# Where the down weights stand in the order of weight loads of a mixture-of-experts loop

## What is computed

```python
def expert_block(args):
    xb, e = args
    hid = jax.nn.silu(xb @ w_gate[e]) * (xb @ w_up[e])
    return hid @ w_down[e]
```

## Time and profile before

| | |
|---|---|
| median of 3 runs | 1393.48 us (1389.54 to 1395.79) |
| profiled execution | 1391.97 us |
| its span | 1389.9 us |
| TensorE matmuls busy | 1292.5 us (93%) |
| VectorE busy | 559.7 us (40%) |
| ScalarE busy | 351.2 us (25%) |
| GpSimd busy | 160.5 us (12%) |
| read from HBM | 299.49 MB |
| down weights, issue to landing, median | 30.5 us |
| gate/up weights, issue to landing, median | 26.8 us |

### The profile page before, as it was taken

The page is one execution under the profiler, slowest core; times in us unless marked ns, Lnnn a source line. Parts: engine busy times, 40 slices in busy tenths (PEclk is TensorE's granted clock), DMA queues, the critical chain, the costliest instruction groups (busy, mean ns, idle before and its releaser), DMA issues.

```text
span 1389.9 us, 21101 instructions
## 1 busy us (share of the span) xinstructions
PE 1292.5 (93%) x7560; PEld 640.0 (46%) x7561; DVE 559.7 (40%) x1034; ACT 351.2 (25%) x759; POOL 160.5 (12%) x278
## 2 busy tenths in 40 slices
PE   5999999999999998999999998999999987897777
PEld 1445656568954444554445545433333333332222
DVE  1366363655214333349786635312212212121115
ACT  1223231422135442221467510101111101110102
POOL 4011010101120000000000001411121111111110
PEclk9999999999999999999999999999999999999999
DMA  9250704323163110014112384789999999999995
GB/s 365 84 212 11 279 26 167 138 79 149 35 187 147 46 46 1 0 49 167 52 57 76 122 348 182 276 350 396 411 412 419 399 406 421 403 402 416 409 391 209
DMA packets 40420, 303.93 MB, mean 219 GB/s; under 512 B 7964, under 2 KB 8116, under 8 KB 22800
## 3 DMA queue, kind: packets, MB, share of 16 engines
q1 hardware_dynamic: 31808, 285.12, 52.3%
q0 software_dynamic: 8528, 17.67, 4.1%
HBM read 299.49 MB, written 13.75 MB: 225 GB/s over the span
## 4 chain that ended last, share of the span: by engine, by line
PE 74%; DMA 14%; DVE 6%; issue 2%; ACT 2%; POOL 1%; DVEq 0%; SPq 0%; ACTq 0%; POOLq 0%
PE bank L858 21%; PE bank L2874 12%; DMA arena<-in_w_down 11%; PE bank L790 8%; PE bank L2892 7%; PE bank L904 4%; PE bank L969 2%; PE bank L847 2%; PE bank L2862 2%; DMA arena<-in_ada_w 1%; PE bank L1186 1%; PE bank L1130 1%; PE bank L1107 1%; PE bank L893 1%; PE bank L2883 1%
## 5 line engine op out<-in xcount | busy, mean ns | idle before, releaser
L858 PE MATMUL bank<-hT,arena 128*128 128x512 f32 x720 | 320.0, 599 | 0.0
L2874 PE MATMUL bank<-arena,hT 128*64 128x512 f32 x1024 | 231.9, 603 | 18.0 <-DMA arena<-in_w_gu 17.6
L858 PEld LDWEIGHTS bank<-hT,arena 128*128 128x128 f32 x720 | 135.0, 191 | 162.6 <-issue 159.2
L2874 PEld LDWEIGHTS bank<-arena,hT 128*64 128x64 f32 x1024 | 72.9, 138 | 156.3 <-issue 138.1
L2892 PE MATMUL bank<-arena,yT 128*64 128x512 f32 x512 | 123.8, 628 | 15.7 <-DMA arena<-in_w_down 13.9
L790 PE MATMUL bank<-arena,yT 128*128 128x512 f32 x256 | 114.5, 601 | 2.4 <-DVE yT L1685 2.3
L3062 DVE TENSOR_SCALAR hT<-hT 128x256 f32<-128x256 f32 x32 | 9.4, 295 | 248.4 <-ACT hT L3000 248.4
L3000 ACT ACTIVATE hT<-bank 128x256 f32<-128x256 f32 x32 | 12.3, 384 | 264.0 <-PE bank L2874 264.0
L790 PEld LDWEIGHTS bank<-arena,yT 128*128 128x128 f32 x256 | 48.1, 192 | 60.0 <-issue 56.2
L2892 PEld LDWEIGHTS bank<-arena,yT 128*64 128x64 f32 x512 | 36.1, 143 | 78.7 <-issue 61.2
L904 PEld LDWEIGHTS bank<-arena 64*64 64x64 f32 x1856 | 59.3, 135 | 23.8 <-issue 14.4
(11 more groups left out here) (489 smaller groups left out, 1609.1 us busy)
## 6 DMA issues: line engine op xcount, KB each, us to landing
arena<-in_w_gu SPq DMA_DIRECT2D x63, 2048.0 KB, 26.8
arena<-in_w_down SPq DMA_DIRECT2D x32, 2048.0 KB, 30.5
arena<-in_w_in SPq DMA_DIRECT2D x53, 512.0 KB, 4.6
arena<-in_ada_w SPq DMA_DIRECT2D x24, 1024.0 KB, 5.1
arena<-in_w_ada SPq DMA_DIRECT2D x8, 1024.0 KB, 9.1
arena<-in_w_out SPq DMA_DIRECT2D x8, 1024.0 KB, 9.0
arena<-in_w_ada SPq DMA_DIRECT2D x8, 512.0 KB, 4.7
arena<-expert_rows SPq DMA_DIRECT2D x4, 1024.0 KB, 8.4
```

Source lines behind the costliest of these rows:

```text
L858: last = T.matmul(bank[0:rows, :], w[:, k, 0:rows], hT[:, k, :], start=k == 0, stop=k == KD - 1)
L2874: last = T.matmul(banks[1 + ub][MT * h:MT * h + MT, :], tile.xT[:, k, :], wgu[u][:, k // 4, k % 4, :, 256 * h:256 * h + 256], start=k == 0 ...
```

## The change

`next_gate_up` gets an argument `between`, which is called after half 0 has been asked for and ahead of the waits for half 1. `body` passes `next_down` there instead of calling it afterwards. Where down already went first (e = 4, 5, 30), nothing moves. For e = 31 there is no next gate/up, and `next_down` is called as before. So SyncE's order in a body is now: half 0 of gate/up of e+1, down of e, half 1 of gate/up of e+1.

```diff
@@ -2701,7 +2701,7 @@
-            def next_gate_up(u, e):
+            def next_gate_up(u, e, between=None):
 
                 p, n = slot_before(e)
                 eng.wait_ge(first.half_done, p + 1)
@@ -2709,6 +2709,8 @@
                 eng.wait_ge(more_.half_done, n + 1)
                 stand_alone(eng)
                 load_half(u, e, 0)
+                if between:
+                    between()
                 eng.wait_ge(first.gate_up, p + 2)
                 stand_alone(eng)
                 eng.wait_ge(more_.gate_up, n + 1)
@@ -2730,10 +2732,10 @@
                 down_first = isinstance(e, int) and (e == NE - 2 or e in (U + 1, U + 2))
                 if down_first:
                     next_down()
-                if not (isinstance(e, int) and e == NE - 1):
-                    next_gate_up(after(it, u)[1], e + 1)
-                if not down_first:
+                if isinstance(e, int) and e == NE - 1:
                     next_down()
+                else:
+                    next_gate_up(after(it, u)[1], e + 1, None if down_first else next_down)
```

## The result

The changed kernel takes 1399.11 us (median of 20 runs, 1393.16 to 1402.87), the kernel before 1393.76 us (20 runs, 1389.54 to 1398.19). The ratio is 1.0040, with a 95% interval of 1.0028 to 1.0052: 5.6 us slower (0.4% of 1394), within 3.9 and 7.3 us. The forecast was 1398.5 us, in a range of 1392.0 to 1404.5 us, with 0.68 on a difference within 0.5%.

The account below looks back on a forecast made before the run. The end is set by when the weight stream delivers its last loads and TensorE's work behind them; 1.3 + 3.4 + 0.9 - 0.5 = 5.1 us over the median of 1393.48 gave 1398.5 us, range 1392 to 1404.5 us.

Parts of the forecast that it names:

- Added delay: Early in the expert loop, later requests for second gate/up halves make the shallow queue lose 1.3 us (0 to 3).
- the first place: Shallow queue early in the loop: down weights of expert 6 land at 964.8 us, due 963.1, a loss of 1.7 us.
- The second place: Shallow queue after the extra tile: down weights of expert 10 land 2.4 us late, the earlier loss included.
- nothing is recovered: After the two shallow spots the queue only deepens, so the stream's lateness stays until the end.
- Order of arrival: At the tail, expert 30's second gate/up half lands after down of 29, so down of 30 starts 3.4 us late.
- The clock: Longer single waits may halve TensorE's clock just ahead of down of 30: 0 to 1.7 us, taken as 0.9.
- the clock decides in every period: Rival: a wait of 3.4 us or more per expert lowers the clock every time, +8 to +12 us; chance 0.22.
- The tail after that: Scatter and reload behind down of 30 start later beside the last weights and gain 0 to 1 us, taken as 0.5.
- Hidden anyway: Rival: expert 30's second gate/up half lands almost with down of 29, 0 to +2 us; chance 0.15.
- A quicker stream: Rival: with fewer loads queued, lagging DMA engines catch up, -6 to -15 us; chance 0.06.
- the shallow places: Two spots early in the loop, one after the extra tile, where the queue runs dry and late requests cost time.
- one of 3 to 4 us per expert: Sign in the profile after 1121 us: TensorE has one such wait for gate/up per expert, almost none for down.

Follow-up runs that it names:

- c1: Control: old order everywhere, with SyncE's loop written as two loops and three bodies; 0.9996 of the kernel before.
- m1: New order for experts 15 to 26 only, old order elsewhere; 0.9991 of the kernel before.
- t2: Old order everywhere except expert 29, which has the new one; 1.0034 of the kernel before.
- s2: Old order for experts 3 and 6 to 14, new order from 15 on; 1.0016 of the kernel before.
- c0: Control: new order everywhere, with SyncE's loop written as two loops and three bodies; 1.0040 of the kernel before.
- t1: New order everywhere except expert 29, which has the old one; 1.0016 of the kernel before.
- s1: New order for experts 3 and 6 to 14 only, old order from 15 on; 1.0009 of the kernel before.
- w1: Changed kernel with 8 idle matmuls ahead of TensorE's wait for the second half of expert 30's gate/up weights; 1.0050 of the kernel before.
- w2: Changed kernel with 4 idle matmuls ahead of TensorE's wait for the second half of expert 30's gate/up weights; 1.0023 of the kernel before.
- d1: New order, with down of both 29 and 30 asked for between the halves of expert 30's gate/up; 1.0080 of the kernel before.
- s3: Old order, but for experts 6 to 14 down is asked for ahead of both halves of the next gate/up; 1.0038 of the kernel before.

## Why the prediction was right, point by point

**The sum held and its terms partly offset each other.** Predicted 1.3 + 3.4 + 0.9 - 0.5 = 5.1 us; measured 5.6 us [3.9, 7.3].

*Added delay, 1.3 us.* Shown for the first place: 1.7 us for D(6), the very figure of the step. The second place was real too. For a measure free of the part ahead of the loop I count from the issue of GU0(7) to the landing of GU0(12): 91.7, 91.1, 91.1, 92.2 and 91.3 us in the five profiles with the old start (before, c1, m1, t2, s2), 94.2, 94.3, 93.7, 93.9, 93.8 and 93.4 us in six with the new one (after, c0, t1, s1, w1, w2; d1, whose tail has another order, gives 94.3 us). That is 2.4 us, where I wrote 2.4 us and took only 1.3 us. To the landing of D(30) the same count gives 401.6, 400.3, 401.4, 401.5, 400.4 against 403.6, 404.4, 401.6, 401.8, 401.7, 401.6 us: 401.0 and 402.5 us on average, 1.4 us. But that rests on two of the new ones, after and c0; the other four lie at most 0.2 us above the highest of the old, and the spread of nearly 3 us among the new ones stays unexplained. So part of the loss may come back, against "nothing is recovered", but these profiles don't settle it, and in s3 nearly all of it stayed. That the taken 1.3 us fits the end is in part luck: my reason for it, that the engine that lands last is less likely to have run dry, was not tested.

*Order of arrival, 3.4 us.* Shown: 9.2 us from the start of the second half to down of 30 in c0 and w2, the switch by one body in t1 and t2, and the double dose in d1.

*The clock, 0.9 us.* Right in kind, too small. Over the five profiles with the late GU1(30) and no idle matmuls (after, c0, t2, s2, d1) the half took 6.54, 3.65, 5.92, 6.32 and 5.63 us: four of five halved, 2.0 us over 3.65 us on average. The upper bound of 1.7 us came from one row; a fall can last through the whole half. This term was mis-sized, as was the gain below, and the two errors partly cancel in the sum. Its rival, that the clock decides in every period, is refuted by m1. The Trainium skill, page "TensorE: Matmul & The Clock Gate", section "HAM oscillation — how this bites in real kernels", says that such a wait at each tile leaves the next tile at the low clock. The trace agrees for five of the six waits of 3.5 us or more in the changed kernel and for none of its four shorter ones (listed at the end); m1 shows that it costs nothing where other waits hide it.

*The tail after that, a gain of 0.5 us.* Too small, and in the changed kernel of another make. From the start of down of 30 to the end of the span took 40.3 us before, and 40.5, 41.1, 40.4, 39.9 and 40.4 us in c1, t1, s1, m1 and s3; with down of 30 late it took 38.5 us in each of after, t2, s2, w1 and d1, and 39.4 and 39.0 us in c0 and w2, where it was less late. In the changed kernel SyncE could ask for the reload 3.9 us after the scatter began (1365.00 to 1368.94 us), not 7.8 us (1355.11 to 1362.90 us) as before; the last weights landed at 1368.7 us, so only 3.7 us of them stood beside it. Then another wait took the place of the reload: VectorE works through expert 31's hidden tile and its check for extra tiles before it adds, and adds from 1376.05 us. In c0 and w2 the chain to the end still runs through scatter and reload, as the prediction had it, and the gain of 0.9 and 1.3 us is theirs. The chain of the changed kernel runs through gate/up of 31 there:

```profile
1347.42 6.54 PE bank L2876 x16
...
1359.51 3.65 PE bank L2894 x16
...
1365.07 7.04 PE bank L2876 x32
...
1372.13 0.39 ACT hT L3002
...
1376.05 1.29 DVE X L3153
```

With these sizes the sum is 1.4 + 3.4 + 2.0 - 1.8 = 5.0 us; 1.4 and 2.0 us are averages over several profiles and 1.8 us compares one pair, so it is a check of size only.

*The rivals.* Hidden anyway fell: the loads arrive in the order of asking, one place apart (GU1(30) at 1347.4 us, D(30) at 1352.3 us). A quicker stream fell too: 410 GB/s before, 409 GB/s in m1's middle. The advice of the Trainium skill, page "DMA: Bandwidth & Descriptors", section "Rules for kernel authors", to issue early was borne out where the prediction said it would be, at the shallow places; the late issues for experts 15 to 26 cost nothing in m1. On the quicker stream the prediction misread its rows: behind the quickest load stand two more, 5.2 and 5.8 us, and 5.3 us is the average of all three. The sign "one of 3 to 4 us per expert" did not come either: the waits run from 0.7 to 4.8 us.

No part of the change that was run alone gained anything clear of the noise: the middle is indifferent, the tail wants the old order, and so, by its trace more than by its time, does the start.

## What to carry to other kernels

In this kernel TensorE is faster than the full queue of loads that feeds it. There the order of requests did nothing to the rate; it decided how much work stood behind the last arrivals, and that was paid once, at the tail. So compare the order of arrival with the order of use for the last few loads, and look at the steps where the queue runs dry, since a few us lost there were still missing 400 us later. One wait that joins several short ones can bring a lower TensorE clock; here that cost only where the work behind it was on the path to the end.

## What the runs showed of the hardware that I had not expected

The long waits of the changed kernel alternate with short ones. From 1110 us on the waits for gate/up weights, taken from TensorE's rows in order, are 3.50, 3.97, 1.55, 3.87 us, and after the extra tile 1.02, 4.46, 0.66, 4.83, 1.84, 4.09 us. Behind 3.97, 3.87, 4.46, 4.83 and 4.09 us the half of 3.65 us took 6.62, 5.35, 6.56, 5.35 and 6.54 us; behind 3.50 us and all the shorter ones it kept 3.65 us. Three of them in full:

```profile
1282.54 6.56 PE L2876 MATMUL bank<-arena,hT 128*64 128x512 f32 x16 [4.46 <-DMA arena<-in_w_gu]
...
1298.32 3.65 PE L2876 MATMUL bank<-arena,hT 128*64 128x512 f32 x16 [0.66 <-DMA arena<-in_w_gu]
...
1315.36 5.35 PE L2876 MATMUL bank<-arena,hT 128*64 128x512 f32 x16 [4.83 <-DMA arena<-in_w_gu]
```

That a slowed stage shortens the next wait, and the short wait lets the clock stay up, fits these rows, but was not tested; s2's are alike. It is no rule: in c0, the same order, three halves in a row were slowed, two of them behind waits of 3.00 and 2.18 us.

```profile
1299.04 5.00 PE L2889 MATMUL bank<-arena,hT 128*64 128x512 f32 x16 [4.22 <-DMA arena<-in_w_gu]
...
1315.61 5.25 PE L2889 MATMUL bank<-arena,hT 128*64 128x512 f32 x16 [3.00 <-DMA arena<-in_w_gu]
...
1331.61 5.35 PE L2889 MATMUL bank<-arena,hT 128*64 128x512 f32 x16 [2.18 <-DMA arena<-in_w_gu]
```

The next wait, 2.04 us ahead of the last half of all, brought no fall there, where the changed kernel had 4.09 us and a fall of 2.9 us. So whether the last expert meets a slow or a fast stage differs from one execution to the next, and the length of the wait alone doesn't tell it.

The time from issue to landing says little about a transfer under a full queue. That D(30) needed 26.7 us from issue to landing in the changed kernel and 32.8 us before went with a landing 2.7 us later (1352.3 against 1349.6 us), at the same rate of the stream: it was asked for 8.8 us later, into a queue that was shorter by 6.1 us.
